# Modulation tiles of a two-layer trunk: four ahead of the first norm, the rest behind projection products

## The chip, the core and the metric

The kernel runs on one core of a Trainium2 chip. PE multiplies matrices into PSUM, DVE, ScalarE (ACT) and GpSimd (POOL) work on SBUF, the first two on PSUM too, and SP issues the transfers; each runs a program of its own, in order, and the programs meet by semaphores that one raises and another waits for. The metric is the time of one execution on the device in microseconds; lower is better.

## The reference, cut to what matters

Two groups of tokens, 1024 sample tokens and 256 prompt tokens, go through the same two layers of width 1024. Each has its own condition (`c`, `c_ctx`). A layer turns the condition into six vectors of 1024, which scale, shift and gate it:

```python
def adaln(cond, w, b):
    m = jax.nn.silu(cond) @ w + b
    return [t[:, None, :] for t in jnp.split(m, ADA_CHUNKS, axis=-1)]
...
        sh1, sc1, g1, sh2, sc2, g2 = adaln(cond, lp['ada_w'], lp['ada_b'])
        h = rmsnorm(x, lp['norm1']) * (1 + sc1) + sh1
...
        x = x + g1 * y
        h = rmsnorm(x, lp['norm2']) * (1 + sc2) + sh2
        x = x + g2 * conv_glu(h, lp, rows)
```

`w` is 1024 x 6144 for each layer, float32, so the modulation reads 50 MB. The mixer of layer 0 is a gated delta rule beside a pooling, that of layer 1 a long convolution; `conv_glu` projects to 2 x 2816 channels (a and gate), convolves a on the 16 x 64 grid of the tokens, and projects gelu(a) times gate down again.

## The kernel before

**Layout.** All 1280 tokens lie along the free axis, channels on the partitions: `XT` is 8 blocks of 128 channels. Weights and activations of the projections are split in a high and a low part; `product` (L590) makes of one 128 x 128 weight block nine matmuls (three pairs of parts, three token chunks of 512, 512, 256). A weight tile is eight such blocks (`k` = 0 to 7), 72 matmuls.

**The front.** SP loads the small vectors, then the token tiles (`load_x`, ten of 128 tokens, six slots) and 24 modulation tiles, each 512 columns of `ada_w` for all 1024 rows (2 MB), in a ring of four slots `AW`. PE transposes the token tiles and for each modulation tile runs eight matmuls of the condition (32 columns wide) against 512 weight columns, L403, spread over four column strips (`LANES`); DVE copies the rows, L419, and PE turns them into columns, L409. DVE then adds the bias into `MOD` (L425) and makes the scales `SCALE_A` (L431 to L438).

**The norm** (`norm`). ScalarE squares `XT` by blocks, GpSimd adds the squares (L530), PE sums over the partitions with a matrix of ones (L480), ScalarE takes the root (L495) and DVE the reciprocal of 1280 columns (L509). For each block DVE multiplies by scale and reciprocal (L516), ScalarE adds the shift (L501) and rounds to the high part (L504), and GpSimd (L534), or for three blocks DVE (L521), makes the low part. PE starts on block k as soon as its low part is there (`h_ready`). Two weight tiles are split ahead (`early`).

**A weight ring** (`weight_ring`). SP loads a tile into one of two raw slots (`load`, L556), ScalarE copies the high part (`hi`, L567), GpSimd subtracts for the low part (`lo`, L573); both parts have two slots. A raw slot is free when both copies are made, a part's slot when PE has used the tile two before.

**The mixer's projection** (`mixer_even`). Twenty tiles: four for the pooling, then k, q, v, z. SP's program holds, in order, the two first weight loads, the store of `XT` to memory, a wait for the end of the norm, small loads (L662 to L665), and then weight loads alternating with the loads of the inverse window lengths (L669), which wait for DVE's pooling of the tile before. ScalarE empties PSUM (L748, L753); its program and the clearing of two buffers by DVE (L780, L781) begin when the norm has ended. From tile 7 on PSUM bank 6 takes sums for the l2 norms (L690).

**The feed-forward** (`conv_glu`). 22 pairs of tiles, a and g, and after every three or four pairs four down tiles d (`items`). For an a tile ScalarE's program waits for PE, copies the result into a padded grid (L1366, L1367), makes the high part of the tile after next, waits for DVE's convolution (twelve operations, L1403 to L1414) and takes the gelu in place (L1370). For a g tile it makes the high part of the tile after next, waits for DVE's product of gelu and gate (L1418) and rounds it (L1374):

```python
                for i, (kind, j, m) in enumerate(items):
                    if kind == "a":
...
                        ring.hi(eng, i + 2, size(i + 2))
                        eng.wait_ge(ve.sem, ve.at("line2", j))
                        eng.activation(CV[j % 2], CV[j % 2], ACT.Gelu_apprx_tanh).then_inc(*ac.did("gelu", j))
                    elif kind == "g":
                        ring.hi(eng, i + 2, size(i + 2))
                        eng.wait_ge(ve.sem, ve.at("hid", j))
```

Of the kernel before, what the change touches and what calls it, by code (L numbers as in the profile page):

```python
# [159 lines left out]
def build(nc, A, OUT):  # L160
    with ExitStack() as ctx:
# [160 lines left out]
        def load_x(r, slots, pairs):  # L322


            XR = [r.take(D) for _ in range(slots)]
            s_x = [sem(f"x_landed{slots}_{i}") for i in range(slots)]
            pe = steps("pe_x", ["lo", "hi"], NT)
            ve = steps("ve_x", ["lo"], NT)
            ac = steps("ac_x", ["hi"], NT)
# [30 lines left out]
        w = Region(W_AT + 1024, ARENA - 256)  # L360
        RAWS = 4
        AW = [w.take(KD, 512) for _ in range(RAWS)]
        w = Region(HT_AT, HT_AT + KD * N)
        AR = [w.take(512) for _ in range(2)]
        w = Region(HT_AT + KD * N, FIX_AT)
        x_steps, x_fetch, x_turn, x_low, x_high = load_x(w, 6, (6, 0))
        NA, LANES = 24, 4
# [3 lines left out]
        veM = steps("ve_mod", ["mod0", "mod1"] + [f"plus{i}" for i in range(4)] + [f"scale{i}" for i in range(5)])  # L371
# [20 lines left out]
        def _(pe):  # L392
            pe.wait_ge(ve00.sem, ve00.at("wide"))
            for n in range(NA + 1):
                if n < NT:
                    x_turn(pe, n)
                if n < NA:
                    pe.wait_ge(s_aw[n % RAWS], 16 * (n // RAWS + 1))
                    if n >= 2:
                        pe.wait_ge(veR.sem, veR.at("rows", n - 2))  # L400
                    for k in range(KD):
                        lane = k % LANES
                        m = pe.matmul(PS[32 * lane:32 * lane + 32, 2 + n % 2, :], CW[:, k, :], AW[n % RAWS][:, k, :], start=k < LANES, stop=k >= KD - LANES)  # L403
                    m.then_inc(*peA.did("rows", n))
                if n:
                    pe.wait_ge(veR.sem, veR.at("rows", n - 1))
                    for j in range(4):
                        c = (4 * (n - 1) + j) * 2
                        m = pe.matmul(PS[:, 4, c:c + 2], AR[(n - 1) % 2][:, j * P:(j + 1) * P], SEL, start=True, stop=True)  # L409
                    m.then_inc(*peT0.did("turn", n - 1))  # L410

        @program("ve")
        def _(ve):
            for n in range(NA + 1):
                if n:
                    ve.wait_ge(peA.sem, peA.at("rows", n - 1))
# [1786 lines left out]
        def x_here(eng, k):  # L2203
            ended(eng, *x_steps)
# [150 lines left out]
```

## Time and profile before

| | |
|---|---|
| median of three runs | 4694.48 us (4691.84 to 4698.06) |
| profiled execution | 4689.33 us, span 4687.5 us |
| mean granted clock of TensorE | 0.937 of full speed |
| busy share of PE, weight loads, DVE, ScalarE, GpSimd | 88%, 73%, 52%, 22%, 25% |
| DMA | 280 MB, mean 60 GB/s; 351 GB/s in the first 117 us |

An instruction is known by its line in the kernel (L403), and helpers have one line for all their uses. In the timeline a bracket gives the idle time of the engine ahead of an operation and what ended it. The chain that ended last is followed back from the last instruction, each step to what released it. The granted clock is the share of TensorE's full 2.4 GHz; 0.5 is 1.2 GHz.

### The profile page before, as it was taken

The numbers are of one execution on the slowest core, as the hardware profiler recorded it, in microseconds if no ns is written. First come the engines' busy times: TensorE is split into PE (matmuls) and PEld (weight loads), VectorE is DVE, ScalarE is ACT, GpSimd is POOL, SyncE is SP. The second block draws the span as 40 slices with busy tenths as digits, with TensorE's granted clock in tenths as the row PEclk, the third lists the DMA queues.
The fourth block names the chain that finished last, engine by engine and source line by source line (L and its number), as shares of the span: only waits on it lengthen the run. The fifth ranks groups of instructions, "written<-read, shape, count | busy, mean of one in ns | idle before, by whom it ended". The sixth has DMA issues, their size and how long they took to land.

```text
span 4687.5 us, 50772 instructions
## 1 busy us (share of the span) xinstructions
PE 4110.0 (88%) x21784; PEld 3429.5 (73%) x21784; DVE 2458.4 (52%) x2646; ACT 1017.6 (22%) x1384; POOL 1178.8 (25%) x586
## 2 busy tenths in 40 slices
PE   6699888778697999999959999996677799999998
PEld 3488777777475888888747777775566588888886
DVE  1466155555416444455447666579992454444453
ACT  1234122211213111111133333311111311111112
POOL 1221133333233222222231000012231422222224
PEclk8799799999798999999979999998888899999999
DMA  9511000000111111111122222232221011111111
GB/s 351 206 52 37 33 1 1 1 1 1 72 37 36 37 41 36 41 36 37 36 78 65 83 80 87 80 144 83 100 111 36 23 37 36 37 37 41 38 39 63
DMA packets 265336, 280.44 MB, mean 60 GB/s; under 512 B 9221, under 2 KB 221142, under 8 KB 261623
## 3 DMA queue, kind: packets, MB, share of 16 engines
q1 hardware_dynamic: 265112, 277.18, 17.5%
q8 instruction: 173, 2.83, 0.3%
q14 instruction: 51, 0.42, 0.0%
HBM read 219.48 MB, written 57.67 MB: 59 GB/s over the span
## 4 chain that ended last, share of the span: by engine, by line
PE 70%; DVE 19%; DMA 4%; issue 3%; ACT 2%; POOL 1%; SPq 1%; POOLq 0%; DVEq 0%; ACTq 0%
PE PS L590 52%; DVE piece L1470 8%; PE PS L1538 5%; DVE piece L1019 3%; DMA piece<-in_l_ada_w 2%; PE PS L990 2%; PE PS L991 2%; PE PS L986 2%; DVE piece L516 2%; PE PS L1711 1%; PE PS L702 1%; DMA piece<-hyena_tokens 1%; DVE piece L1406 1%; DVE piece L509 1%; DVE piece L1879 0%
## 5 line engine op out<-in xcount | busy, mean ns | idle before, releaser
L590 PE MATMUL PS<-piece,piece 128*128 128x512 f32 (+1 forms) x13824 | 2757.3, 361 | 150.7 <-POOL piece L534 94.5
L590 PEld LDWEIGHTS PS<-piece,piece 128*128 128x128 f32 x13824 | 2304.4, 190 | 600.7 <-issue 160.7
L573 POOL TENSOR_TENSOR piece<-piece,piece 128x1024 fp32r<-128x1024 f32 (+1 forms) x204 | 504.7, 2475 | 2417.9 <-ACT piece L567 2417.9
L1538 PE MATMUL PS<-piece,piece 128*128 128x256 f32 x1920 | 441.3, 392 | 126.1 <-DVE piece L2165 110.8
L1406 DVE SCALAR_TENSOR_TENSOR piece<-piece,piece,piece 128x1024 f32<-128x1024 f32 x352 | 534.9, 1520 | 12.6
L1538 PEld LDWEIGHTS PS<-piece,piece 128*128 128x128 f32 x1920 | 376.4, 197 | 186.1 <-DVE piece L2165 113.6
L1426 DVE SCALAR_TENSOR_TENSOR piece<-PS,piece,piece 128x1024 f32<-128x1024 f32 x224 | 187.7, 879 | 415.0 <-PE PS L590 415.0
L567 ACT ACTIVATE piece<-piece 128x1024 fp32r<-128x1024 f32 (+1 forms) x204 | 205.1, 1007 | 671.4 <-PE PS L590 634.5
L1019 DVE TENSOR_TENSOR piece<-piece,PS 128x512 f32<-128x512 f32 x288 | 185.3, 684 | 249.6 <-PE PS L991 192.3
L1403 DVE TENSOR_SCALAR piece<-piece,piece 128x1024 f32<-128x1024 f32 x44 | 35.7, 812 | 482.4 <-ACT piece L1367 482.4
L1125 POOL TENSOR_TENSOR piece<-piece,piece 128x512 f32<-128x512 f32 x120 | 159.8, 1345 | 123.9 <-PE PS L986 123.2
L1370 ACT ACTIVATE piece<-piece 128x1280 f32<-128x1280 f32 x44 | 56.1, 1275 | 607.5 <-DVE piece L1414 607.5
L1470 DVE TENSOR_TENSOR piece<-piece 128x512 f32<-128x512 f32 (+2 forms) x168 | 177.0, 1053 | 18.2 <-ACT piece L2130 11.1
L986 PE MATMUL PS<-piece,piece 128*128 128x128 f32 x960 | 138.2, 288 | 49.6 <-DVE piece L1019 42.8
L1470 DVE SCALAR_TENSOR_TENSOR piece<-piece 128x512 f32<-128x512 f32 (+1 forms) x288 | 165.1, 573 | 9.9
L986 PEld LDWEIGHTS PS<-piece,piece 128*128 128x128 f32 x960 | 119.1, 195 | 65.5 <-DVE piece L1019 56.2
L1258 DVE SCALAR_TENSOR_TENSOR piece<-PS,piece,piece 128x1024 f32<-128x1024 f32 (+1 forms) x32 | 26.8, 879 | 231.8 <-PE PS L590 231.8
L1879 DVE TENSOR_TENSOR piece<-piece,PS 128x512 f32<-128x512 f32 x80 | 52.8, 683 | 178.0 <-PE PS L1711 178.0
L2144 POOL TENSOR_TENSOR piece<-piece,piece 128x512 f32<-128x512 f32 x40 | 56.5, 1412 | 340.4 <-DVE piece L2165 340.4
L1101 ACT ACTIVATE piece<-PS 128x512 f32<-128x512 f32 x120 | 71.7, 597 | 278.3 <-PE PS L986 278.3
L1366 ACT ACTIVATE piece<-PS 128x1024 f32<-128x1024 f32 x44 | 45.3, 1030 | 397.1 <-PE PS L590 397.1
L1386 POOL TENSOR_TENSOR piece<-piece,piece 128x1280 fp32r<-128x1280 f32 x44 | 129.8, 2949 | 2.9 <-ACT piece L1374 2.9
(206 smaller groups left out, 3719.1 us busy)
## 6 DMA issues: line engine op xcount, KB each, us to landing
piece<-in_l_ada_w SPq DMA_DIRECT2D x24, 2048.0 KB, 18.1
piece<-in_l_ffn_up SPq DMA_DIRECT2D x88, 512.0 KB, 3.7
piece<-in_l_w_in SPq DMA_DIRECT2D x44, 512.0 KB, 3.8
piece<-in_l_ffn_down SPq DMA_DIRECT2D x48, 384.0 KB, 3.0
piece<-filters_s SPq DMA_DIRECT2D x8, 2176.0 KB, 10.5
filters_s<-piece SPq DMA_DIRECT2D x64, 256.0 KB, 2.0
hyena_tokens<-piece SPq DMA_DIRECT2D x24, 640.0 KB, 4.0
piece<-hyena_tokens SPq DMA_DIRECT2D x12, 1280.0 KB, 5.7
```

The lines of the kernel that those rows point to most:

```text
L516: eng.scalar_tensor_tensor(T[k % 4][:, a:a + n], XT[:, k, a:a + n], SCALE_A[:, which, k, j:j + 1], RS[:, a:a + n], ALU.mult, ALU.mult).the ...
L567: eng.activation(HI[i % 2][0][:, 0:n], RAW[i % raws][:, 0:n], ACT.Copy).then_inc(*self.ac.did("hi", i))
L573: eng.tensor_tensor(LO[i % 2][0][:, 0:n], RAW[i % raws][:, 0:n], HI[i % 2][1][:, 0:n], ALU.subtract)\
L590: m = eng.matmul(PS[:, bank + b, 0:n], w, x[:, a:a + n], start=first and n_ == 0, stop=last and n_ == 2)
L986: heads(d, 0, lambda o, hd: eng.matmul(o, lm[:, hd, :], bf["Y"][:, hd, :], start=True, stop=True)).then_inc(*pe.did(f"r{v}", it))
L1019: eng.tensor_tensor(out, a, b, op).then_inc(*ve.did(step, it))
L1125: eng.tensor_tensor(bf[f"M{v % 2}"], bf["L"], over(LVM[:, d, v, :], HEADS), ALU.mult).then_inc(*po.did(f"lm{v}", it))
L1386: eng.tensor_tensor(hl, CV[j % 2], hh, ALU.subtract).then_inc(*po.did("lo", j))
L1406: eng.scalar_tensor_tensor(acc, src, w, acc, ALU.mult, ALU.add).then_inc(*ve.did(f"grid{k}", j))
L1426: eng.scalar_tensor_tensor(XT[:, mm, a:a + n], PSF[:, at_:at_ + n], MOD[:, layer, 40 + mm, c:c + 1], XT[:, mm, a:a + n], ALU.mult, ALU.add ...
L1470: f(*args).then_inc(*st.did(f"{tag}{n[0]}", rnd))
L1538: m = eng.matmul(PS[:, bank, o * HC:(o + 1) * HC], M[i][o], rhs[i], start=i == 0, stop=i == 1)
```

## The change

The front loads and multiplies four modulation tiles only (shift and scale of the first norm), behind token tiles 2, 5, 7 and 9. The squares of the tokens are taken by ScalarE from the raw token tiles, and DVE sums them along the channels, which gives one number for each token on its partition (`SS`, 128 x 10). A norm of its own, `first_norm`, takes root and reciprocal of these, spreads them on a diagonal, and lets PE's matrix of ones bring them to all partitions; the result stays in PSUM, where DVE's multiplication reads it.

Nine tiles more (eight of layer 0, the first of layer 1) become 18 half tiles of 256 columns in the mixer's projection: three for each of its first six weight tiles, behind blocks 0, 3 and 5, with two slots `BW`; the columns of half h are turned behind the rows of half h + 1, and ScalarE copies the rows at the head of the item. The last eleven tiles, of layer 1, become 44 quarters of 128 columns in the feed-forward of layer 0: one for every a and every g tile, its rows behind block 1, its column behind block 6, one slot `QW`; ScalarE copies the rows at the head of the item. The feed-forward's weight ring has one raw slot in place of two, in both layers. DVE makes the rest of `MOD` and `SCALE_A` at mixer tile 6 and ahead of the last down tiles.

```diff
+            ve = steps("ve_x", ["lo", "sum"], NT)
+            ac = steps("ac_x", ["square", "hi"], NT)
...
             def fetch(eng, t):
                 if t >= slots:
                     eng.wait_ge(pe.sem, pe.at("hi", t - slots))
+                    eng.wait_ge(ac.sem, ac.at("square", t - slots))
...
             def low_channels(eng, t):
...
+                eng.wait_ge(ac.sem, ac.at("square", t))
+                eng.tensor_reduce(SS[:, t:t + 1], SQX[t % 2], AX.X, ALU.add).then_inc(*ve.did("sum", t))
...
             def high_channels(eng, t):
+                eng.wait_ge(s_x[t % slots], 16 * (t // slots + 1))
+                if t >= 2:
+                    eng.wait_ge(ve.sem, ve.at("sum", t - 2))
+                eng.activation(SQX[t % 2], XR[t % slots], ACT.Square).then_inc(*ac.did("square", t))
...
-        NA, LANES = 24, 4
+        NA, LANES = 4, 4
+        ADA_BEHIND = (2, 5, 7, 9)
...
         @program("sp")
         def _(sp):
-            for t in range(3):
-                x_fetch(sp, t)
             for n in range(NA):
-                if 3 <= n < NT:
-                    x_fetch(sp, n)
-                if n >= RAWS:
-                    sp.wait_ge(peA.sem, peA.at("rows", n - RAWS))
-                layer, m = divmod(n, 12)
-                src = A[f"l{layer}_ada_w"].rearrange("(p k) n -> p k n", k=KD)[:, :, m * 512:(m + 1) * 512]
+                for t in ((0, 1, 2), (3, 4, 5), (6, 7), (8, 9))[n]:
+                    x_fetch(sp, t)
+                src = A["l0_ada_w"].rearrange("(p k) n -> p k n", k=KD)[:, :, n * 512:(n + 1) * 512]
                 sp.dma_start(AW[n % RAWS], src).then_inc(s_aw[n % RAWS], 16)
...
+            for t in range(NT):
+                x_turn(pe, t)
+                if t in ADA_BEHIND:
+                    n = ADA_BEHIND.index(t)
+                    rows(n)
+                    if n:
+                        columns(n - 1)
+            columns(NA - 1)
...
-            ve.tensor_copy(SCALE_A[:, 4], bcast(vec("final_norm", 0, 8), 2)).then_inc(*veM.did("scale4"))
+            ve.tensor_tensor(MOD[:, 0, 0:16], PS[:, 4, 0:32].rearrange("p (m j) -> p m j", j=2), bcast(vec("l0_ada_b", 0, 16), 2), ALU.add)\
+                .then_inc(*veM.did("mod"))
+            ve.wait_ge(veM.sem, veM.at("mod"))
+            ve.tensor_scalar(SCALE_A[:, 0], MOD[:, 0, 8:16, :], 1.0, None, ALU.add).then_inc(*veM.did("plus"))
+            ve.wait_ge(veM.sem, veM.at("plus"))
+            ve.tensor_tensor(SCALE_A[:, 0], SCALE_A[:, 0], bcast(vec("l0_norm1", 0, 8), 2), ALU.mult).then_inc(*veM.did("scale"))
+            ve.tensor_copy(SCALE_A[:, 4], bcast(vec("final_norm", 0, 8), 2)).then_inc(*veM.did("last"))
...
+        def first_norm(prev, shift, early):
+
+            T = [Region(W_AT + i * N, W_AT + (i + 1) * N).take(N) for i in range(4)]
+            DIAG = Region(FIX_AT - N, FIX_AT).take(NT, P)
+            RS = psum(3, N)
...
+            @program("pe")
+            def _(eng):
+                eng.wait_ge(ve.sem, ve.at("diag"))
+                for b, (a, n) in enumerate(CHUNKS):
+                    m = eng.matmul(PS[:, 3 + b, 0:n], ones, DIAG[:, a // P:(a + n) // P, :].rearrange("p t c -> p (t c)"), start=True, stop=True)
+                m.then_inc(*pe.did("sum"))
...
+            @program("ac")
+            def _(eng):
+                ended(eng, *prev)
+                eng.activation(SS, SS, ACT.Sqrt, scale=1.0 / D, bias=eps).then_inc(*ac2.did("root"))
+                early["ac"](eng)
...
+            @program("ve")
+            def _(eng):
+                eng.wait_ge(ac2.sem, ac2.at("root"))
+                ended(eng, *prev)
+                eng.reciprocal(SS, SS).then_inc(*ve.did("inv"))
+                eng.wait_ge(ve.sem, ve.at("inv"))
+                eng.tensor_tensor(DIAG, over(ident, NT), bcast(SS, P), ALU.mult).then_inc(*ve.did("diag"))
+                eng.wait_ge(pe.sem, pe.end())
...
+                        for (a, n, j), g in zip(GROUPS, "sp"):
+                            eng.scalar_tensor_tensor(T[k % 4][:, a:a + n], XT[:, k, a:a + n], SCALE_A[:, 0, k, j:j + 1], RS[:, a:a + n],
+                                                     ALU.mult, ALU.mult).then_inc(*ve2.did(f"{g}{k}"))
...
+            NB, PER, ADA_TILES = 2 * (13 - NA), 3, 7
...
+            def halves(i):
+                return [h for h in range(PER * i, PER * (i + 1)) if h < NB]
+
+            def fetch_half(eng, h):
+                if h >= 2:
+                    eng.wait_ge(peB.sem, peB.at("rows", h - 2))
+                layer, m = divmod(NA + h // 2, 12)
+                at = m * 512 + h % 2 * 256
+                eng.dma_start(BW[h % 2], A[f"l{layer}_ada_w"].rearrange("(p k) n -> p k n", k=KD)[:, :, at:at + 256]).then_inc(s_aw[h % 2], 16)
+
+            def half_rows(eng, h):
+                eng.wait_ge(s_aw[h % 2], 16 * (h // 2 + 2))
+                if h >= 2:
+                    eng.wait_ge(acBr.sem, acBr.at("rows", h - 2))
+                for k in range(KD):
+                    lane = k % LANES
+                    m = eng.matmul(PS[32 * lane:32 * lane + 32, 6 + h % 2, 0:256], CW[:, k, :], BW[h % 2][:, k, :], start=k < LANES, stop=k >= KD - LANES)
+                m.then_inc(*peB.did("rows", h))
+
+            def half_columns(eng, h):
+                eng.wait_ge(acBr.sem, acBr.at("rows", h))
+                for j in range(2):
+                    c = 256 + 4 * (h // 2) + 2 * j
+                    m = eng.matmul(PS[:, 6 + h % 2, c:c + 2], BR[h % 2][:, j * P:(j + 1) * P], SEL, start=True, stop=True)
+                m.then_inc(*peBt.did("turn", h))
...
+            def half_leaves(eng, h):
+                eng.wait_ge(peB.sem, peB.at("rows", h))
+                if h >= 2:
+                    eng.wait_ge(peBt.sem, peBt.at("turn", h - 2))
+                eng.activation(BR[h % 2], PS[:, 6 + h % 2, 0:256], ACT.Copy).then_inc(*acBr.did("rows", h))
...
+            def modulation(eng):
+                eng.wait_ge(peBt.sem, peBt.end())
...
             @program("sp")
             def _(eng):
-                ended(eng, *before_norm)
                 for i, (kind, g, at) in enumerate(tiles):
                     ring.load(eng, i, w_in[:, :, at:at + P], (KD, P))
+                    if i >= 2:
+                        for h in halves(i - 2):
+                            if h + 2 < NB:
+                                fetch_half(eng, h + 2)
                     if i == 1:
+                        ended(eng, *before_norm)
+                        fetch_half(eng, 0)
+                        fetch_half(eng, 1)
                         eng.dma_start(spill, XT).then_inc(s_spill, 16)
                         ended(eng, *prev)
...
+                            if n == 0:
+                                ended(eng, veB)
...
+                        if k == KD - 1:
+                            m.then_inc(*pe.did("used", i))
+                        h = {0: 0, 3: 1, 5: 2}.get(k)
+                        if h is not None and PER * i + h <= NB:
+                            h += PER * i
+                            if h < NB:
+                                half_rows(eng, h)
+                            if h:
+                                half_columns(eng, h - 1)
...
                 for i, (kind, g, _) in enumerate(tiles):
+                    for h in halves(i):
+                        half_leaves(eng, h)
+                    if i == ADA_TILES - 1:
+                        ended(eng, peB, peBt)
...
+                    if 4 + i == ADA_TILES - 1:
+                        modulation(eng)
...
-            ring = weight_ring(r, len(items))
+            ring = weight_ring(r, len(items), 1)
...
+            NQ, Q_CHUNK = (2 * KH, 4) if layer == 0 else (0, 0)
...
+            def quarter(kind, j):
+                return 2 * j + (kind == "g")
...
                     ring.load(eng, i, src, shape(items[i]))
+                    if i and items[i - 1][0] in "ag" and NQ:
+                        q = quarter(*items[i - 1][:2])
+                        if q:
+                            eng.wait_ge(peQ.sem, peQ.at("rows", q - 1))
+                        at = (Q_CHUNK + q) * P
+                        eng.dma_start(QW, A["l1_ada_w"].rearrange("(p k) n -> p k n", k=KD)[:, :, at:at + P]).then_inc(s_aw[2], 16)
...
-                        m.then_inc(*pe.did("used", i))
+                            if k == KD - 1:
+                                m.then_inc(*pe.did("used", i))
+                            q = quarter(kind, j)
+                            if k == 1 and NQ:
+                                eng.wait_ge(s_aw[2], 16 * (q + 2))
+                                for kk in range(KD):
+                                    lane = kk % LANES
+                                    m = eng.matmul(PS[32 * lane:32 * lane + 32, 6 + q % 2, 0:P], CW[:, kk, :], QW[:, kk, :], start=kk < LANES, stop=kk >= KD - LANES)
+                                m.then_inc(*peQ.did("rows", q))
+                            if k == KD - 2 and NQ:
+                                eng.wait_ge(acQ.sem, acQ.at("rows", q))
+                                at_ = P + 2 * (q // 2)
+                                eng.matmul(PS[:, 6 + q % 2, at_:at_ + 2], QR[q % 2], SEL, start=True, stop=True).then_inc(*peQt.did("turn", q))
...
                 for i, (kind, j, m) in enumerate(items):
+                    if kind in "ag" and NQ:
+                        q = quarter(kind, j)
+                        eng.wait_ge(peQ.sem, peQ.at("rows", q))
+                        if q >= 2:
+                            eng.wait_ge(peQt.sem, peQt.at("turn", q - 2))
+                        eng.activation(QR[q % 2], PS[:, 6 + q % 2, 0:P], ACT.Copy).then_inc(*acQ.did("rows", q))
                     if kind == "a":
...
+                    if kind == "d" and j == len(GROUPS_OF) - 1 and mp == 0 and NQ:
+                        eng.wait_ge(peQt.sem, peQt.end())
...
+                            eng.tensor_tensor(out, two, bcast(bias, 2), ALU.add).then_inc(*veQ.did(f"mod{odd}"))
...
         before, early = prev, {}
-        prev, h_ready = norm(prev, x_here, HL_END, 0, mod(0, 0), early)
+        prev, h_ready = first_norm(prev, mod(0, 0), early)
```

## Rows read from the trace of the kernel before

**Rows 1.** Chain that ended last, shares of the span by line.

```profile
PE PS L590 52%; DVE piece L1470 8%; PE PS L1538 5%; DVE piece L1019 3%; DMA piece<-in_l_ada_w 2%; PE PS L990 2%; PE PS L991 2%; PE PS L986 2%; DVE piece L516 2%; PE PS L1711 1%; PE PS L702 1%; DMA piece<-hyena_tokens 1%; DVE piece L1406 1%; DVE piece L509 1%; DVE piece L1879 0%
```

**Rows 2.** The chain in order of time: start us, us on it, what.

```profile
157.93 3.60 PE PS L403 x16
...
209.74 94.23 PE PS L590 x486
...
1460.15 845.22 PE PS L590 x4338
```

**Rows 3.** Timeline from 0 us: start, us, engine, line, operation, count, idle before.

```profile
23.23 3.64 PE L403 MATMUL PS<-piece,piece 128*32 128x512 f32 x16 [4.38 <-DMA piece<-in_l_ada_w]
...
28.65 1.92 PE L403 MATMUL PS<-piece,piece 128*32 128x512 f32 x16
...
30.51 1.05 PE L409 MATMUL PS<-piece,piece 128*128 128x2 f32 x8
...
48.34 3.23 PE L403 MATMUL PS<-piece,piece 128*32 128x512 f32 x16 [1.22 <-DMA piece<-in_l_ada_w]
...
55.04 1.92 PE L403 MATMUL PS<-piece,piece 128*32 128x512 f32 x16 [1.23 <-DMA piece<-in_l_ada_w]
```

**Rows 4.** Timeline of the first norm and the first weight tile.

```profile
165.42 3.80 PE L480 MATMUL PS<-piece,piece 128*128 128x512 f32 x6 [2.02 <-DVE piece L438]
...
171.98 8.15 DVE L509 RECIPROCAL piece<-piece 128x1280 f32<-128x1280 f32 x1 [7.13 <-ACT piece L495]
...
180.17 11.76 DVE L516 SCALAR_TENSOR_TENSOR piece<-piece,piece,piece 128x1024 f32<-128x1024 f32 x8
...
201.79 5.80 PE L590 MATMUL PS<-piece,piece 128*128 128x512 f32 x18 [1.11 <-POOL piece L534]
...
211.34 0.37 SPq L662 DMA_DIRECT2D piece<-in_l_pool_w  x1
...
213.04 1.15 DVE L781 MEMSET piece<- 128x1304 f32 x1 [0.22 <-issue]
...
219.94 1.06 ACT L567 ACTIVATE piece<-piece 128x1024 fp32r<-128x1024 f32 x1 [4.26 <-DMA piece<-in_l_w_in]
```

**Rows 5.** DMA issues: count, KB each, median us from issue to landing.

```profile
piece<-in_l_ada_w SPq DMA_DIRECT2D x24, 2048.0 KB, 18.1
...
hyena_tokens<-piece SPq DMA_DIRECT2D x24, 640.0 KB, 4.0
piece<-hyena_tokens SPq DMA_DIRECT2D x12, 1280.0 KB, 5.7
```

**Rows 6.** Timeline of the third and fourth weight tile's ends.

```profile
241.36 1.30 ACT L748 ACTIVATE piece<-PS 128x1024 f32<-128x1024 f32 x2 [11.67 <-PE PS L590]
...
251.22 0.33 SPq L669 DMA_DIRECT2D piece<-in_k_inv  x1
...
255.28 1.30 ACT L748 ACTIVATE piece<-PS 128x1024 f32<-128x1024 f32 x2 [11.48 <-PE PS L590]
```

**Rows 7.** Timeline of the feed-forward's first tiles.

```profile
1462.14 1.26 DVE L1391 MEMSET piece<- 128x1446 f32 x1 [0.56 <-DVE piece L521]
...
1491.96 1.03 ACT L1366 ACTIVATE piece<-PS 128x1024 f32<-128x1024 f32 x1 [7.69 <-PE PS L590]
1492.88 0.38 ACT L1367 ACTIVATE piece<-PS 128x256 f32<-128x256 f32 x1
...
1508.11 1.27 ACT L1370 ACTIVATE piece<-piece 128x1280 f32<-128x1280 f32 x1 [13.90 <-DVE piece L1414]
...
1519.96 1.03 ACT L1366 ACTIVATE piece<-PS 128x1024 f32<-128x1024 f32 x1 [7.75 <-PE PS L590]
```

**Rows 8.** Waits of 1460 to 2306 us: us, times, longest.

```profile
ACT piece L1370 <- DVE piece L1414: 289.8, 21, 14.0
```

**Rows 9.** Windows: stretch, length, busy us per engine, granted clock, DMA share, GB/s.

```profile
2329.00:2333.00 4.00, 3.82 (x12) 3.18 (x13) 0.00 (x0) 0.00 (x0) 0.08 (x1) 0.58 0.05 14
```

**Rows 10.** Timeline at that stretch; in brackets the pause before.

```profile
2329.18 57.98 PE L590 MATMUL PS<-piece,piece 128*128 128x512 f32 x288 [9.82 <-issue]
```

More of the change, by code:

```diff
@@ L325, in load_x @@
             XR = [r.take(D) for _ in range(slots)]
+            SQX = [r.take(D) for _ in range(2)]
             s_x = [sem(f"x_landed{slots}_{i}") for i in range(slots)]
             pe = steps("pe_x", ["lo", "hi"], NT)
-            ve = steps("ve_x", ["lo"], NT)
-            ac = steps("ac_x", ["hi"], NT)
+            ve = steps("ve_x", ["lo", "sum"], NT)
+            ac = steps("ac_x", ["square", "hi"], NT)
             def bank(t):
@@ L393, in _, with rows @@
             pe.wait_ge(ve00.sem, ve00.at("wide"))
[L394 to L410, printed above, removed]
+            def rows(n):
+                pe.wait_ge(s_aw[n % RAWS], 16 * (n // RAWS + 1))
+                if n >= 2:
+                    pe.wait_ge(veR.sem, veR.at("rows", n - 2))
+                for k in range(KD):
+                    lane = k % LANES
+                    m = pe.matmul(PS[32 * lane:32 * lane + 32, 2 + n % 2, :], CW[:, k, :], AW[n % RAWS][:, k, :], start=k < LANES, stop=k >= KD - LANES)
+                m.then_inc(*peA.did("rows", n))
@@ new lines, in columns @@
+            def columns(n):
+                pe.wait_ge(veR.sem, veR.at("rows", n))
+                for j in range(4):
+                    c = (4 * n + j) * 2
+                    m = pe.matmul(PS[:, 4, c:c + 2], AR[n % 2][:, j * P:(j + 1) * P], SEL, start=True, stop=True)
+                m.then_inc(*peT0.did("turn", n))
+            for t in range(NT):
[5 more added lines that the diff above has]
+                        columns(n - 1)
@@ L412, in _, with rows @@
+            columns(NA - 1)
         @program("ve")
         def _(ve):
[L414 to L421 removed]
+            def rows(n):
+                ve.wait_ge(peA.sem, peA.at("rows", n))
+                if n >= 2:
+                    ve.wait_ge(peT0.sem, peT0.at("turn", n - 2))
+                ve.tensor_copy(AR[n % 2], PS[:, 2 + n % 2, :]).then_inc(*veR.did("rows", n))
@@ L422, in _ @@
+            for t in range(NT):
+                x_low(ve, t)
+                if t in ADA_BEHIND:
+                    rows(ADA_BEHIND.index(t))
             ve.wait_ge(peT0.sem, peT0.end())
             ve.wait_ge(ac0.sem, ac0.at("cols1"))
-            for layer in range(2):
-                ve.tensor_tensor(MOD[:, layer], PS[:, 4, 96 * layer:96 * layer + 96].rearrange("p (m j) -> p m j", j=2),
-                                 bcast(vec(f"l{layer}_ada_b", 0, 48), 2), ALU.add).then_inc(*veM.did(f"mod{layer}"))
@@ L427, in _ @@
-            ve.wait_ge(veM.sem, veM.at("mod1"))
-            for i in range(4):
-                layer, second = divmod(i, 2)
-                at = 8 + 24 * second
-                ve.tensor_scalar(SCALE_A[:, i], MOD[:, layer, at:at + 8, :], 1.0, None, ALU.add)\
-                    .then_inc(*veM.did(f"plus{i}"))
-            ve.wait_ge(veM.sem, veM.at("plus3"))
-            for i in range(4):
-                layer, second = divmod(i, 2)
-                ve.tensor_tensor(SCALE_A[:, i], SCALE_A[:, i], bcast(vec(f"l{layer}_norm{second + 1}", 0, 8), 2),
-                                 ALU.mult).then_inc(*veM.did(f"scale{i}"))
@@ L633, in mixer_even @@
             ring = weight_ring(ring_at, n_t)
+            NB, PER, ADA_TILES = 2 * (13 - NA), 3, 7
+            BW = [Region(W_AT + 5248 + 2048 * i, W_AT + 5248 + 2048 * (i + 1)).take(KD, 256) for i in range(2)]
+            BR = [Region(W_AT + 9344 + 256 * i, W_AT + 9344 + 256 * (i + 1)).take(256) for i in range(2)]
+            peB, peBt = steps("pe_ada", ["rows"], NB), steps("pe_ada_turn", ["turn"], NB)
+            acBr = steps("ac_ada_half", ["rows"], NB)
+            veB = steps("ve_mod", ["mod00", "mod01", "mod10", "mod11"] + [f"{t}{i}" for t in ("plus", "scale") for i in range(1, 2)])
```

96 lines of the change are left out of this document (80 added, 16 removed).

## The prediction

> **What bounds the kernel now.** I read the page's chain by line first: the split matrix products (`product`, L590) carry 52% of the span, and the loads of the modulation weights 2% [rows 1]. The chain in order of time says where that lies. Up to 157.93 us it is a row of loads; then come the last modulation rows, the first norm, and from 209.74 us PE runs weight tiles without a gap; from 1460.15 us it does so for 845 us through the feed-forward of layer 0 [rows 2]. So the front is bound by loads, and both projections into which the change moves work are bound by PE. A load taken off the front is worth its full time; a matmul added behind it costs its full time, and any wait that the added work puts into PE's queue costs more. The page's run took 4689.33 us for a span of 4687.5; the median of the three runs is 5.15 us above that. A difference of 0.2%, some 9 us, is about what a measurement of this kernel can tell from none.
>
> **The front: a gain of 117 us.** 24 tiles of 2.097 MB become 4, with the same ten token tiles of 0.524 MB. Before the first modulation product, at 23.23 us, three token tiles and one weight tile have landed (3.67 MB). Then one weight and one token tile, 2.62 MB, take 55.04 - 48.34 = 6.70 us, which is 0.391 MB per us [rows 3]. The other 9.96 MB of the new front need 25.5 us, so the fourth tile's product starts at 48.7 where the 24th now starts at 157.93 [rows 2]: 109.2 us earlier. ScalarE's new squares (about 1.06 us each, as the copy of the same 1024 elements in rows 4, plus its channel copy) come to under 20 us for ten tiles and hide under these loads; so do DVE's ten sums.
>
> The norm behind it changes too. Now PE's sum starts at 165.42, the reciprocal of 1280 columns takes 8.15 us and the first multiplication starts at 180.17: 14.8 us [rows 4]. After, the table load and a root of 10 columns (1.7, an estimate from the 2.7 us between the sum's end and the reciprocal), a reciprocal of 10 columns (0.2), a diagonal of 1280 elements (1.5, from 11.76/8 per operation), the same PE sum (3.8) and the signals between them come to 7.8. Ahead of the sum, between the end of the last rows at 161.53 and 165.42, eleven small operations become four; I take 1 us for that. 8 us are saved. From that multiplication on the norm keeps its pace, bound by DVE, ScalarE and GpSimd in turn. The front saves 109.2 + 8.0 = 117.2.
>
> **The first weight tile: a loss of 15 us.** In old times: PE has done six of its eight steps at 201.79 + 5.80 = 207.6, and the tile ends at 209.74 plus two steps, 213.2. The change puts half tile 2 behind step 5. Its load stands on SP's queue behind the wait for the whole norm, which ends at about 211.2 (SP's next issue is at 211.34), then five small issues and a weight load. That weight load has landed only at 219.94, when ScalarE's copy starts [rows 4]. 1 MB behind it takes 2.7 us more at the rate above: 222.6. Alone, between 640 KB in 4.0 and 1280 KB in 5.7 us [rows 5], it would be 5 us from its issue near 214.9, so 219.9. I take 222. PE also stops earlier: the columns of half 0, at step 3, need a copy that ScalarE makes only after DVE's clearing, at 213.04 + 1.15 = 214.2 [rows 4]. From 214.2 the two steps left up to half 2 at half clock reach 220.5, so both waits end together. Behind 222 come the rows and columns (2.5 us at half clock) and two steps (3.5): the tile ends at 228, 14.8 late, with 12 to 18 as bounds.
>
> **The other half tiles: 28 us.** A 512-column tile takes 1.92 us at full clock for its 8 products, and its four column turns 1.05 [rows 3]. Half as many columns and turns: 1.1 + 0.5, and 0.1 for the change of operands, 1.7 each. 15 halves and one last turn cost 26. None hides: PE has no gap there. SP issues the loads in order behind the window loads: in weight tile 3 the issue of its inverse comes 9.9 us after the tile before ended (251.22 against 241.36, rows 6), the half behind it lands 6 us later, and PE wants it at 13.8 us (six steps and two halves): 2 us more. The rest land in time. ScalarE's and DVE's parts fall into waits for PE of over 11 us [rows 6].
>
> **The quarters: a loss of 185 us.** This decides. Two weight tiles, a and g, take 1519.96 - 1491.96 = 28.0 us [rows 7], so a tile takes 14.0 and a step 1.75. Behind step 1 of each come the quarter's 8 products of 128 columns (0.7 us, a quarter of 1.92 and 0.2 to fill), behind step 6 the turn of one column (0.26, from 1.05/4), and that turn waits for ScalarE's copy of the rows. ScalarE runs its program in order, and the copy stands at the head of each item. For a that is early. For g it stands behind the gelu of the same pair, and the gelu waits for DVE's convolution: 21 waits, 289.8 us, up to 14.0 each [rows 8]. From the end of a (1491.96) to the end of the gelu (1508.11 + 1.27) it is 17.4 us [rows 7]. The copy, 128 columns against 0.38 us for 256 [rows 7], makes 17.75 with its signals. PE has done seven steps and the rows at 12.25 + 0.7 = 12.95. It stands still for 4.8 us in every pair, and behind this wait stands all of PE's queue.
>
> After such a pause PE runs slower: in the first 4 us after a pause of 9.8 us the granted clock was 0.58 [rows 9, 10], which is 1.2 GHz for most of it, and the 8 products at 23.23 us, after a pause of 4.4, took 3.64 us where others took 1.92 [rows 3]. Step 7, 1.75 us, then takes 1.7 more. A pair lasts 17.75 + 0.3 + 1.75 + 1.7 for g and 14.0 + 1.05 for a: 36.55 against 28.05, 8.5 more. DVE starts the next convolution only when the next a ends, so nothing is won back. 21 such pairs cost 178.5. In the last pair PE waited already, and only g's later end counts, 4. In the first tile ScalarE is held by the clearing until 1463.4 [rows 7]: 2.2. Together 185.
>
> The Trainium skill warns of such pauses in TensorE: Matmul & The Clock Gate, section Why this matters for your kernels: gaps between bursts of matmuls put the engine back to half rate. The trace agrees with its 0.58 [rows 9]. By the rule every pair pays the 1.7 us; without it the sum is 37 us lower, the first of the rivals.
>
> **One raw slot.** A load now waits for both copies of the tile before it. A tile lasts 14 us, and a load of 512 KB under the 4.0 of 640 KB [rows 5], so it lands in time. In the norms' early part, with only the old reciprocal's 8 us to cover it, it is close: I take 1 for both layers, 0 to 4. The later modulation sums sit in DVE's waits: 0.
>
> **Sum.** -117.2 + 14.8 + 26 + 2 + 185 + 1 = +111.6: 4801 on the profiled run, 4806 on the median. I say 4803.
>
> **Rivals.**
>
> *The clock stays up.* The pauses are 4.8 us between long busy stretches, and a pause of 1.23 us cost nothing (1.92 at 55.04, rows 3). Then 22 x 1.7 = 37 less: 4766. Against it: the longer pauses of [rows 3, 10].
>
> *The copy isn't late (the other side).* If ScalarE got to g's copy before PE's step 7, within 13 us of a's end, the quarters would cost 44 x 1.05 = 46 and the change would gain: -117 + 43 + 46 + 1 = -27, 4665. It decides at 4.8 us: the convolution and gelu would have to end that much sooner. Nothing in the change shortens them, so this needs an order on ScalarE other than the one I read.
>
> *Inserts are dearer.* The 1.92 us rest on four column strips working at once. If short products in strips did not overlap, a quarter's rows cost up to 1 us more on the 22 a tiles and a half's up to 2.3 on 15: +57, 4860. For: no row shows such short ones. Against: [rows 3] show strips followed by full-width turns without a gap (28.65 + 1.92 against 30.51).
>
> The Trainium skill, TensorEngine Tiling (Array Packing), section Key Properties, says that a change of tiling mode drains the array; each insert makes two. The trace shows no gap for it, so by the trace it adds nothing; by the rule it would go to this rival.
>
> *It doesn't do what it says.* If the halves' loads took the 18.1 us of the front [rows 5] and not 5, every half would wait about 5 us, the two slots being spaced 12.8: +75, 4878. Against: that figure belongs to a full queue.
>
> **How the numbers follow.** Forecast 0.70, clock up 0.12, not late 0.06, dearer 0.08, late loads 0.04. The forecast alone spans 4778 to 4833 (first tile -3 to +3, raw slot, quarters' rows 0.5 to 1.1, clock loss 1.0 to 1.9). The range takes in the clock rival and most of the dearer one: 4750 to 4858. Faster by over 0.2% is the third case but for its upper edge, 0.05; within 0.2% 0.02; slower 0.93.
>
> **What would show it.** PE's steady start near 93 us; one pause of 14 to 15 us in two parts inside the first tile; in the feed-forward of layer 0 an idle of about 4.8 us per pair ended by ScalarE's copy, the clock down behind it, pairs of 36 us, and that stage from 846 to about 1030 us; layer 1's feed-forward unchanged. The prediction is wrong if PE in that stage has no such pause, if the pause is not followed by half clock, or if the front ends later than 100 us.

## The result and the profile after

The changed kernel takes 4834.32 us (median of four runs, 4825.98 to 4845.93), the kernel before 4696.27 beside it: 1.0295 times as long, with an interval of 1.0271 to 1.032. The profiled execution took 4837.13 us for a span of 4835.3, which is 147.8 us more than the profiled one of before. The forecast was 4803 with 4750 to 4858 as range.

The front, on PE's timeline (start us, us, engine, line and operation, count, in brackets the idle time before and what ended it). L404 are the rows of the first modulation tiles, L666 the products of the weight tiles: 27 of these matmuls, called 27 products below, are three steps of nine:

```profile
49.36 2.38 PE L404 MATMUL PS<-piece,piece 128*32 128x512 f32 x16 [3.32 <-DMA piece<-in_l_ada_w]
...
93.84 1.01 PE L740 MATMUL PS<-piece,piece 128*128 128x2 f32 x4 [9.65 <-ACT piece L747]
...
102.29 1.07 PE L733 MATMUL PS<-piece,piece 128*32 128x256 f32 x16 [2.14 <-DMA piece<-in_l_ada_w]
...
123.85 1.07 PE L733 MATMUL PS<-piece,piece 128*32 128x256 f32 x16 [2.64 <-DMA piece<-in_l_ada_w]
...
125.32 7.02 PE L666 MATMUL PS<-piece,piece 128*128 128x512 f32 x27
...
148.04 1.93 PE L733 MATMUL PS<-piece,piece 128*32 128x256 f32 x16 [3.73 <-DMA piece<-in_l_ada_w]
...
150.78 8.08 PE L666 MATMUL PS<-piece,piece 128*128 128x512 f32 x27
158.79 1.07 PE L733 MATMUL PS<-piece,piece 128*32 128x256 f32 x16
159.79 0.61 PE L740 MATMUL PS<-piece,piece 128*128 128x2 f32 x4
160.26 5.46 PE L666 MATMUL PS<-piece,piece 128*128 128x512 f32 x27
...
176.37 1.94 PE L733 MATMUL PS<-piece,piece 128*32 128x256 f32 x16 [5.52 <-DMA piece<-in_l_ada_w]
```

On the same view, DVE's first multiplications of the norm and SP's first issue behind its end:

```profile
64.41 6.42 DVE L597 SCALAR_TENSOR_TENSOR piece<-piece,piece,PS 128x1024 f32<-128x1024 f32 x8 [4.73 <-PE PS L567]
...
90.35 0.37 SPq L801 DMA_DIRECT2D piece<-in_l_pool_w  x1
```

The fourth modulation tile starts at 49.36 where [rows 2] had the 24th at 157.93. The issue behind the norm stands at 90.35 where [rows 4] had it at 211.34: 121 us earlier. Then the half tiles (L733 rows, L740 columns) give time back: one pause of 9.65 us for ScalarE's copy, and four for loads. Behind the two longest of the loads' (3.73 and 5.52 us), the rows take 1.93 us instead of 1.07. Behind the first of these two the 27 products that follow take 8.08 instead of 5.46; behind the one of 2.64 us they take 7.02.

The feed-forward of layer 0 on the same view, first of PE (L666 product, L1513 a quarter's rows, L1518 its column), then of ScalarE:

```profile
1413.18 8.98 PE L666 MATMUL PS<-piece,piece 128*128 128x512 f32 x45
1426.85 0.59 PE L1518 MATMUL PS<-piece,piece 128*128 128x2 f32 x2 [4.69 <-ACT piece L1548]
1427.29 8.12 PE L666 MATMUL PS<-piece,piece 128*128 128x512 f32 x27
1435.34 0.64 PE L1513 MATMUL PS<-piece,piece 128*32 128x128 f32 x16
1435.91 8.97 PE L666 MATMUL PS<-piece,piece 128*128 128x512 f32 x45
1444.73 0.28 PE L1518 MATMUL PS<-piece,piece 128*128 128x2 f32 x2
1444.86 5.49 PE L666 MATMUL PS<-piece,piece 128*128 128x512 f32 x27
```

```profile
1446.90 1.03 ACT L1554 ACTIVATE piece<-PS 128x1024 f32<-128x1024 f32 x1 [10.58 <-PE PS L666]
...
1463.03 1.27 ACT L1558 ACTIVATE piece<-piece 128x1280 f32<-128x1280 f32 x1 [13.88 <-DVE piece L1616]
1464.20 0.26 ACT L1548 ACTIVATE piece<-PS 128x128 f32<-128x128 f32 x1
```

The gelu (L1558) waits for DVE's convolution, the copy of the quarter (L1548) starts as the gelu ends, and PE has stood for 4.69 us when the copy is made. The waits from 1400 to 2500 us (us in total, times, longest) count 23 such, those of the 22 g tiles and one of 1.78 us in the first a tile. The windows behind one of them give the clock (the 1.00 or 0.50 after the engines' busy times; 0.50 is 1.2 GHz):

```profile
PE PS L1518 <- ACT piece L1548: 103.3, 23, 4.8
```

```profile
1426.80:1428.80 2.00, 1.96 (x6) 1.76 (x7) 0.00 (x0) 0.00 (x0) 0.00 (x0) 0.50 0.00 0
1428.80:1430.80 2.00, 2.00 (x7) 1.61 (x7) 0.00 (x0) 0.00 (x0) 0.00 (x0) 0.50 0.00 0
1430.80:1432.80 2.00, 2.00 (x8) 1.61 (x7) 1.49 (x1) 1.39 (x2) 0.73 (x1) 0.50 0.00 0
1432.80:1434.80 2.00, 2.00 (x11) 1.73 (x11) 0.00 (x0) 0.94 (x1) 2.00 (x2) 0.93 0.00 0
1434.80:1444.00 9.20, 9.20 (x61) 7.49 (x60) 0.00 (x0) 0.28 (x1) 2.57 (x1) 1.00 0.40 114
```

By stages, the profiled execution after against the one of before:

| stage | forecast us | measured us |
|---|---|---|
| front and first norm | -117.2 | -121 |
| first weight tile | +14.8 | +15 |
| the other half tiles | +28 | +46 |
| mixer behind the projection | 0 | +1 |
| feed-forward of layer 0 | +185 | +203 |
| mixer of layer 1 | 0 | +5 |
| the rest | +1 | -1 |

The first three end where PE begins the small products of 16 columns behind the projection (435.8 us, 495.8 before): 60 us ahead. At the end of layer 0 it is 144 us behind. Layer 1's mixer took 1181.2 us from the start of ScalarE's last square in the norm ahead of it to the first product of its second projection, 1176.5 before. In the six kernels below the same stretch, in which they change nothing, took 1174.8 to 1181.3. So the 5 us are taken for scatter between executions.

### The profile page after: what moved, and what is told of

It is laid out like the page before. It is cut to its first block, busy times and chain, and to the rows that moved or that the text cites. A ratio compares the mean times of both kernels' runs of the same rounds, so it can differ in the third digit from the quotient of the medians.

```text
span 4835.3 us, 52247 instructions
## 1 busy us (share of the span) xinstructions
PE 4173.5 (86%) x22456; PEld 3490.6 (72%) x22456; DVE 2452.7 (51%) x2642; ACT 1033.9 (21%) x1448; POOL 1155.5 (24%) x579
## 4 chain that ended last, share of the span: by engine, by line
PE 64%; DVE 24%; issue 4%; DMA 3%; ACT 2%; POOL 1%; SPq 0%; DVEq 0%; POOLq 0%; ACTq 0%
PE PS L666 46%; DVE piece L1672 7%; DVE piece L1608 6%; PE PS L1740 5%; DVE piece L1174 3%; PE PS L1145 2%; PE PS L1146 2%; PE PS L1141 2%; DMA piece<-in_l_ada_w 1%; PE PS L1913 1%; DVE piece L521 1%; PE PS L851 1%; DMA piece<-hyena_tokens 1%; DVE piece L1616 0%; DVE piece L2109 0%
## 5 line engine op out<-in xcount | busy, mean ns | idle before, releaser
L666 PE MATMUL PS<-piece,piece 128*128 128x512 f32 (+1 forms) x13824 | 2837.0, 366 | 133.3 <-POOL piece L539 74.1
L666 PEld LDWEIGHTS PS<-piece,piece 128*128 128x128 f32 x13824 | 2347.0, 194 | 599.4 <-issue 161.3
L1740 PEld LDWEIGHTS PS<-piece,piece 128*128 128x128 f32 x1920 | 375.4, 197 | 185.0 <-DVE piece L2367 113.9
L1558 ACT ACTIVATE piece<-piece 128x1280 f32<-128x1280 f32 x44 | 56.0, 1272 | 607.9 <-DVE piece L1616 607.9
L1141 PEld LDWEIGHTS PS<-piece,piece 128*128 128x128 f32 x960 | 119.3, 195 | 65.6 <-DVE piece L1174 56.3
L1620 DVE TENSOR_TENSOR piece<-piece,PS 128x1280 f32<-128x1280 f32 x44 | 65.5, 1488 | 153.3 <-PE PS L666 123.8
```

Source lines behind the costliest of these rows:

```text
L666: m = eng.matmul(PS[:, bank + b, 0:n], w, x[:, a:a + n], start=first and n_ == 0, stop=last and n_ == 2)
L1141: heads(d, 0, lambda o, hd: eng.matmul(o, lm[:, hd, :], bf["Y"][:, hd, :], start=True, stop=True)).then_inc(*pe.did(f"r{v}", it))
L1740: m = eng.matmul(PS[:, bank, o * HC:(o + 1) * HC], M[i][o], rhs[i], start=i == 0, stop=i == 1)
```

## The experiments

My theory was the forecast's: the loss is the 21 pauses, each the wait for a copy that stands behind the gelu, with half clock behind it. The rivals that the traces left open: that the inserted products themselves, or the switch of operands, are dear; and that the clock falls for another reason than the pause. The first two experiments part these.

**The copy ahead of the gelu.** ScalarE makes g's copy within a's item, before it waits for the convolution; all else stays.

```diff
-                    if kind in "ag" and NQ:
-                        q = quarter(kind, j)
+                    def quarter_copy(q):
...
+                    if kind == "a" and NQ:
+                        quarter_copy(quarter("a", j))
...
                        ring.hi(eng, i + 2, size(i + 2))
+                        if NQ:
+                            quarter_copy(quarter("g", j))
                        eng.wait_ge(ve.sem, ve.at("line2", j))
```

> Only ScalarE's copy of g's quarter rows moves: from the head of item g to the place in item a ahead of the wait for the convolution. Theory (the copy is late because it stands behind the gelu): PE's wait at the quarter's column turn, 103.3 us in 23 waits, goes to under 5 us, the clock stays up, a pair falls from 37.67 to about 30.0 us (28.05 and two inserts of 1.0), and the kernel falls by about 157 us from 4834 to about 4677. Rival one (the quarter's weights land late, or the inserts themselves are dear): the place of the copy changes nothing, pairs stay near 37.7 and the time near 4834. Rival two (the moved copy blocks ScalarE ahead of the gelu by as much): the pause moves to the gelu and less than half comes back, about 4760.

Measured: 4673.92 us, where 4677 was expected, and 0.9966 of the kernel before (0.9953 to 0.9978). ScalarE's timeline and the windows of the stage:

```profile
1409.12 0.38 ACT L1556 ACTIVATE piece<-PS 128x256 f32<-128x256 f32 x1
...
1412.29 0.28 ACT L1547 ACTIVATE piece<-PS 128x128 f32<-128x128 f32 x1 [1.85 <-PE PS L1513]
...
1424.33 1.27 ACT L1561 ACTIVATE piece<-piece 128x1280 f32<-128x1280 f32 x1 [10.46 <-DVE piece L1619]
...
1439.00 0.38 ACT L1556 ACTIVATE piece<-PS 128x256 f32<-128x256 f32 x1
```

```profile
1407.00:2290.00 883.00, 883.00 (x5086) 736.20 (x5086) 411.01 (x369) 152.67 (x194) 222.33 (x87) 1.00 0.21 61
```

The copy now stands 12 us ahead of the gelu, PE is busy for all of 883 us, and its clock is 1.00. A pair takes 1439.00 - 1409.12 = 29.88 us against 28.0 [rows 7]: so four inserts (two rows, two columns) cost 1.9 us. The place of one copy is worth 160 us, and it turns the change from a loss into a gain.

**The pause filled.** 22 products that nothing reads stand ahead of g's wait, so that PE works through part of the pause; the copy stays late.

```diff
                             if k == KD - 2 and NQ:
+                                for _ in range(22 if kind == "g" else 0):
+                                    eng.matmul(PS[:, 6, 256:512], w[0][:, k, :], HH[:, 0, 0:256], start=True, stop=True)
                                 eng.wait_ge(acQ.sem, acQ.at("rows", q))
```

> The kernel after, with 22 further matmuls of 256 columns in each g tile of layer 0's feed-forward, put on PE just ahead of the wait for the late copy; their result goes to an unused part of PSUM and nobody reads it. They take about 4.3 us of the 4.7 us pause. Theory (the pause costs twice, once as idle time and again as half clock behind it): the granted clock stays at 1.0, the step behind the pause and the first two steps of the next tile run at full speed, a pair falls by about 2.9 us and the kernel by about 64 us to about 4770, although PE does more work. Rival (the slow step has another cause, or the added work is simply added): the clock still falls to 0.5 and the time stays within 10 us of 4834 or goes above it.

Measured: 4798.73 us (two runs), ratio 1.0231 (1.0199 to 1.0264): some 36 us better, where 64 were expected. PE's timeline in two pairs:

```profile
1423.63 2.77 PE L1517 MATMUL PS<-piece,piece 128*128 128x256 f32 x22
1428.48 0.38 PE L1520 MATMUL PS<-piece,piece 128*128 128x2 f32 x2 [2.08 <-ACT piece L1550]
1428.72 5.50 PE L666 MATMUL PS<-piece,piece 128*128 128x512 f32 x27
...
1940.72 2.77 PE L1517 MATMUL PS<-piece,piece 128*128 128x256 f32 x22
1945.65 0.38 PE L1520 MATMUL PS<-piece,piece 128*128 128x2 f32 x2 [2.16 <-ACT piece L1550]
1945.90 7.06 PE L666 MATMUL PS<-piece,piece 128*128 128x512 f32 x27
```

The 22 products were expected to take 4.3 us; they took 2.77 and left pauses of 1.6 to 2.2. Behind these the next 27 products took 5.5 us in ten of the first 21 pairs and 6.8 to 7.1 in the other eleven, the third pair among them (the expectation of the next run puts the first four pairs at 5.5; that is so for three of them). Either a pause of some 2 us still lowers the clock at times, or something else does. So the next run filled nearly all of it.

**The pause filled further.** The same edit with 36 products.

> As the kernel with 22 extra products ahead of g's column wait, but with 36 of them (256 columns each, into a part of the bank that nothing reads). There the 22 took 2.77 us, 126 ns each, and left a pause of 2.1 us; behind it 27 products took 5.5 us in the first four pairs, but 6.8 to 7.1 in about half of the later ones. 36 take 4.5 us and leave about 0.3. Theory (the pause sets back the clock, and a pause short enough doesn't): the 27 products take 5.5 us behind every pause, the granted clock is 1.00 through the stage, each pair of layer 0's feed-forward takes 34.9 us instead of 37.2, and the time is 4834 less 22 times 2.6, about 4775. Rival (something else than the pause, the inserted products or the turn of a column for instance, lowers the clock): the 27 products still take about 7 us in part of the pairs, and the time stays near 4799. If the extra products cost PE time themselves the pair grows above 34.9 and the time above 4799.

Measured: 4779.18 us, ratio 1.0202 (1.0185 to 1.0219), where 4775 was expected.

```profile
1455.12 4.43 PE L1517 MATMUL PS<-piece,piece 128*128 128x256 f32 x36
1459.98 0.38 PE L1520 MATMUL PS<-piece,piece 128*128 128x2 f32 x2 [0.43 <-ACT piece L1550]
1460.23 5.49 PE L666 MATMUL PS<-piece,piece 128*128 128x512 f32 x27
```

```profile
1450.00:2400.00 950.00, 943.02 (x5625) 797.47 (x5624) 396.44 (x358) 146.45 (x184) 213.57 (x84) 1.00 0.19 55
```

The pause is 0.43 us here and at most 0.51 elsewhere, 27 products take 5.5 behind each of the first 21, and the clock is 1.00 over 950 us, with the same inserts in the same places. So the pause is what lowers the clock, not the inserts. Why pauses of some 2 us lowered it in some pairs and not in others stays open. The run also parts the loss in two: about 55 us are the clock (4834.32 against 4779.18). The late copy itself still holds the pair at 34.9 us (29.9 with the copy in time) and costs the larger part.

**The halves' loads one place earlier.** SP loads three halves behind each weight load, and the first of the three is the half that PE takes last in a weight tile, behind block 5. From tile 1 on (counted from 0) SP now issues it one place earlier: ahead of its wait for the pooling, the inverse (L808) and the next weight load (L632), and no longer behind them. The expectation calls it the first half; it is the first in SP's order.

```diff
-                        for h in halves(i - 2):
-                            if h + 2 < NB:
-                                fetch_half(eng, h + 2)
+                        for h in range(2 if i == 2 else PER * (i - 1), PER * i):
+                            if h < NB:
+                                fetch_half(eng, h)
```

> Only the order on SP changes in the mixer's projection: the load of the first half tile of each weight tile is issued one place earlier, ahead of the inverse window's load and of the next weight load instead of behind both. Theory (the halves land late because they wait behind DVE's pooling and behind 1.2 MB in the queue): the pauses of 2.6, 3.7 and 5.5 us at the second to fourth weight tile go, with the half clock behind them, and the projection ends about 15 us earlier: about 4819. Rival (a half's load is slow in itself, 8 to 9 us from issue whatever stands ahead): landing times stay at 8 us or more and at least half of the pauses stay, 4827 to 4834.

Measured: 4813.01 us, where about 4819 was expected, ratio 1.0262 (1.024 to 1.0284). The interval overlaps that of the change; the trace is plainer. PE's waits from 90 to 440 us of the change, then of this kernel:

```profile
PE PS L733 <- DMA piece<-in_l_ada_w: 14.0, 4, 5.5
PE PS L740 <- ACT piece L747: 9.6, 1, 9.6
```

```profile
PE PS L740 <- ACT piece L747: 9.8, 1, 9.8
PE PS L733 <- DMA piece<-in_l_ada_w: 2.4, 1, 2.4
```

Three of the four waits for loads are gone, 11.6 us, and the projection ends 21.3 us earlier (414.5 against 435.8): the other 10 us are mostly the half clock behind those pauses, for the rows now take 1.07 us and 27 products 5.46 in every one of these tiles. The loads' median fell from 8.2 to 6.4 us. The half behind block 5 of tile 1 is issued at 109.92 instead of 114.94 and lands 5.4 us later instead of 8.9. So the edit moves the issue and frees the queue ahead of it; no run parts the two.

**The first tile.** SP issues halves 2 and 3 before its wait for the norm, ScalarE makes the first copies before its own wait for it, and PE takes columns 0, rows 2 and columns 1 behind the last block.

```diff
                         eng.dma_start(spill, XT).then_inc(s_spill, 16)
+                        fetch_half(eng, 2)
+                        fetch_half(eng, 3)
                         ended(eng, *prev)
...
-                        h = {0: 0, 3: 1, 5: 2}.get(k)
+                        h = ({0: 0, 3: 1, 7: 2} if i == 0 else {0: 0, 3: 1, 5: 2}).get(k)
...
+                            if h == 2:
+                                half_columns(eng, 0)
...
+                for h in halves(0):
+                    half_leaves(eng, h)
                 ended(eng, *prev)
```

> Only the first weight tile's inserts change: SP loads half tiles 2 and 3 ahead of its wait for the end of the norm, ScalarE makes the first three copies ahead of its own wait for the norm and the clearing, and PE makes the columns of halves 0 and 1 and the rows of half 2 behind the tile's last block. Theory (the two waits for the norm's end cost the first tile 15 us): the pauses of 9.7 and 2.1 us inside the first tile go, it ends about 13 us earlier, and the kernel falls to about 4821. Rival (the norm still sets the pace and the time is lost again at the second tile's halves): less than 5 us.

Measured: 4821.89 us, where about 4821 was expected, ratio 1.0281 (1.026 to 1.0303). Whole runs don't separate this from the change, whose interval is 1.0271 to 1.032. In the trace the 9.6 us wait for ScalarE's copy is gone, 12.9 us of waits for loads stay, and the projection ends at 420.5, 15.3 us earlier.

**All three together.**

> The kernel after with three moves at once and nothing left out: g's quarter copy ahead of the gelu, the halves' loads ahead of the inverse window's, and the first tile's inserts behind its last block with their loads and copies ahead of the waits for the norm. Theory (the three losses are separate and add): 157 + 15 + 13 us less than 4834, so about 4649, which is 1.0% below the kernel before. Rival (they are one and the same slack, or DVE and GpSimd become the bound in the projection): the gains do not add and the time stays above 4690.

Measured: 4638.46 us, where about 4649 was expected, and 0.9888 of the kernel before (0.9872 to 0.9905): 1.1% faster than it. PE's waits from 90 to 440 us:

```profile
PE PS L733 <- DMA piece<-in_l_ada_w: 0.2, 1, 0.2
```

By the profiled spans the three edits alone save 162.9, 26.9 and 18.0 us, 208 in sum; together they save 199. This kernel beats both.

## Why the prediction was right, and where it was off

**Direction, mechanism, range: right.** The time lies 31 us above the forecast and inside the range, and the term that was said to decide it does. The range was part luck: the forecast alone was said to span 4778 to 4833, the time lies 1 us above that, and it is held by the room left for a rival (dearer inserts) that is out. On the profiled executions the sum was +111.6 and the change +147.8: the half tiles and the quarters cost 18 us each more than their terms, layer 1's mixer shows 5 us of scatter, and the front gave 4 more.

**The front: right.** -121 for -117.2. The fourth tile starts at 49.36 (48.7 by the sum). From that tile to the first multiplication the norm saved 7.2 us for the 8 forecast. But "from that multiplication on the norm keeps its pace" was wrong: up to SP's issue behind the norm it takes 25.9 us (64.41 to 90.35) for 31.2 (180.17 to 211.34). The first eight multiplications take 6.42 us for the 11.76 of [rows 4], and single rows show why, first of the kernel before, then of the changed one:

```profile
184.81 6.84 POOL L534 TENSOR_TENSOR piece<-piece,piece 128x1280 fp32r<-128x1280 f32 x2 [7.19 <-ACT piece L504]
188.80 3.13 DVE L516 SCALAR_TENSOR_TENSOR piece<-piece,piece,piece 128x256 f32<-128x256 f32 x1
```

```profile
69.05 5.80 POOL L610 TENSOR_TENSOR piece<-piece,piece 128x1280 fp32r<-128x1280 f32 x2 [4.86 <-ACT piece L582]
69.17 1.27 DVE L597 SCALAR_TENSOR_TENSOR piece<-piece,piece,PS 128x1024 f32<-128x1024 f32 x1
```

Six of the eight take the same in both kernels, 1.27 to 1.28 us for 1024 columns and 0.48 for 256. The last two of the kernel before, with all operands in SBUF, ran beside GpSimd's subtractions (L534) and took 3.93 and 3.13; those of the changed kernel, with the norm in PSUM, took 1.27 and 0.47 beside GpSimd (L610). So the pace of a multiplication didn't change: it is no longer held up beside GpSimd.

**The first weight tile: right**, 15 for 14.8, in two waits as reckoned: 9.65 us for the copy, two slow steps (5.44), then 2.14 for the load. The waits are 11.8 us in all, less than the pause of 14 to 15 us that the prediction names as a sign.

**The other half tiles: the term for late loads was mis-sized**, +46 for 28. Inserts were right (1.07 + 0.61 for 1.7). But "the rest land in time" was wrong: I counted one late load of 2 us and 5 to 6 us for a load, from rows of single transfers [rows 5]. SP's timeline shows what they meet:

```profile
114.07 0.33 SPq L808 DMA_DIRECT2D piece<-in_k_inv  x1
114.50 0.39 SPq L632 DMA_DIRECT2D piece<-in_l_w_in  x1
114.94 10.57 SPq L725 DMA_DIRECT2D piece<-in_l_ada_w  x3
```

The half issued at 114.94 stands behind two loads issued 0.4 and 0.9 us before; PE's rows at 123.85 had waited for it, 8.9 us. Three tiles pay 2.64, 3.73 and 5.52, in all 11.9 us for 2; half clock behind them costs another 9, which the sum had left out. The earlier issue gave back 21.3 us, which agrees with both together.

**The quarters: the pause was right, the clock term mis-sized.** The pause was forecast at 4.8 and is 4.69; a pair without clock loss was forecast at 34.85 and takes 34.9 with the pause filled. Inserts alone were put at 2.1 us a pair; with the copy in time they measured 1.9. The loss by the clock was put at 1.7 us a pair, from the few products of one step; but the half clock lasts longer than that step: 27 products behind a pause take 8.0 to 8.2 us in the first four pairs and 7.3 to 8.0 later, for 5.49, which is 1.8 to 2.7 us. ScalarE's first and last grid copy, before and after, bound 21 pairs:

```profile
1464.04 1.03 ACT L1366 ACTIVATE piece<-PS 128x1024 f32<-128x1024 f32 x1 [5.12 <-PE PS L590]
...
2305.40 1.03 ACT L1366 ACTIVATE piece<-PS 128x1024 f32<-128x1024 f32 x1 [7.69 <-PE PS L590]
```

```profile
1409.23 1.03 ACT L1554 ACTIVATE piece<-PS 128x1024 f32<-128x1024 f32 x1 [2.34 <-PE PS L666]
...
2444.22 1.03 ACT L1554 ACTIVATE piece<-PS 128x1024 f32<-128x1024 f32 x1 [10.57 <-PE PS L666]
```

They grew by 193.6 us, 9.2 each for the forecast 8.5; with the pause filled by 36 products they grew by 142.0, so the clock cost 2.5 a pair. The fault was to let the slow stretch end with step 7; the row at 2329 [rows 9] covers 4 us only.

**One raw slot: right.** No wait of PE for the weight ring shows in either feed-forward, and layer 1's, with one slot and no quarters, takes 843.49 us on the chain that ended last, for 846.76 before.

**The rivals.** *The clock stays up* is out: 0.50 for some 6 us behind the first long pause, and slow products behind all 21. *The copy isn't late* gave 4665 as a price, and the kernel in which it is not late took 4673.92, so the price was right and only the case was not this one. *Inserts are dearer* is out: L1513 takes 0.64 us, L733 1.07. *Late half loads* was right for three halves of the 15, as a cost of 21 us and not of 75.

The Trainium skill's TensorE: Matmul & The Clock Gate, section Why this matters for your kernels, warns that gaps between bursts put the engine back to half rate. The trace agrees: pauses of 4.2 to 4.8 us did in all 21 pairs. It goes further too, for pauses of 1.6 to 2.2 us, shorter than those that the Trainium skill warns of there, did in eleven pairs of 21 (27 products in 7.06 us behind one), while 0.5 us and less never did.

## What to carry to other kernels

Before a small step goes into the queue of the engine that bounds a stage, follow its result through the engine in between: what stands ahead of it in that engine's order, and when does that end? Here one copy a place too late cost 160 us, three times the 51 us by which the best version gains on the kernel before. A pause is priced as its length plus what the stretch at half clock behind it costs, and here that stretch outlasted the step that waited; a load is priced with what is issued just ahead of it.

## What the runs showed of the hardware

- Behind the first pause of 4.7 us PE ran at half clock for some 6 us (0.50 in three windows of 2 us, 0.93 in the fourth); behind all 21 (4.2 to 4.8 us) 27 products lost 1.8 to 2.7 us. Behind 1.6 to 2.2 us they were slow in eleven pairs and not in ten, with the same program; behind 0.5 us and less never.
- The loads of 1 MB took 8.2 us in the median with the halves behind the inverse and the weight load, and 6.4 with one in three issued ahead of them; those of 512 KB took 3.7 to 5.0.
- DVE's multiplication of 1024 columns took 1.28 us with all operands in SBUF and 3.93 beside a subtraction of GpSimd; with one operand in PSUM it took 1.27 beside GpSimd too (256 columns: 0.48, 3.13, 0.47). The traces show it in place; no run tried it alone.
